# Keys' 32 rotary columns on the four quarters of the output, and the first loads in smaller pieces

## What is computed

```python
h = x @ w_in[l]                       # mla_cq 256, mla_ckv 128, mla_kr 32 columns among them
c = _rmsnorm(ckv, kv_norm)
k_rope = _rope(kr, cos, sin)          # t1*cos - t2*sin, t1*sin + t2*cos, shared by all heads
k = (mem @ w_k).reshape(B, M, MEM_HEADS, MEM_HDIM)
```

## Time and profile before

| what | value |
|---|---|
| runs shown | 1431.75, 1429.74, 1429.59 us; median 1429.74 |
| the profiled execution, its own time | 1432.5 us |
| its span, first to last instruction | 1430.7 us |
| mean granted PE clock | 0.964 |
| PE busy | 1283.5 us, 90% |
| DVE / ACT / POOL busy | 815.5 / 412.4 / 644.0 us |
| bytes moved | 407.8 MB, 268.5 of them by the gather |

### The profile page before, as it was taken

One profiled execution on the slowest core, in us unless ns is written; L12 is line 12 of the kernel. 1 busy time (PEld: TensorE's weight loads), 2 busy tenths in 40 slices (PEclk: granted clock), 3 DMA queues, 4 the chain that ended last, 5 costly groups with the idle time before them and its releaser, 6 DMA issues.

```text
span 1430.7 us, 17532 instructions
## 1 busy us (share of the span) xinstructions
PE 1283.5 (90%) x6312; PEld 790.5 (55%) x6312; DVE 815.5 (57%) x1681; ACT 412.4 (29%) x1032; POOL 644.0 (45%) x643
## 2 busy tenths in 40 slices
PE   9999999999999999999997899958977778787786
PEld 8877686548876686549556556523323333332332
DVE  0766377341566377351438756789797654544555
ACT  0532344111333333221322333322322231212123
POOL 0566667332537666433103344444644454444440
PEclk9999999999999999999999999978988989999999
DMA  9544334265453344365537999999999999999995
GB/s 379 192 163 178 118 141 184 110 262 198 152 184 155 118 177 175 134 229 196 203 151 270 413 419 412 420 420 420 420 419 420 420 421 419 421 420 419 421 420 209
DMA packets 53600, 407.82 MB, mean 285 GB/s; under 512 B 6133, under 2 KB 8586, under 8 KB 10890
## 3 DMA queue, kind: packets, MB, share of 16 engines
q0 software_dynamic: 36864, 268.45, 45.5%
q1 hardware_dynamic: 15562, 137.21, 24.9%
q10 hardware_dynamic: 1088, 1.05, 0.4%
HBM read 404.56 MB, written 1.07 MB: 284 GB/s over the span
## 4 chain that ended last, share of the span: by engine, by line
PE 39%; DMA 24%; DVE 7%; issue 3%; POOL 3%; ACT 3%; ACTq 0%; POOLq 0%; DVEq 0%
PE pj L675 13%; PE bank L1100 10%; DMA ring<-in_peer_uv,vM 9%; PE pj L711 5%; DMA yT<-in_peer_uv,vM 5%; DMA hv<-in_peer_uv,vM 3%; PE pj L690 3%; DMA more_rows<-in_peer_uv,vM 3%; DMA qM<-in_peer_uv,vM 3%; PE pj L970 2%; POOL more_rows L598 1%; DVE tri L1852 1%; PE bank L644 1%; POOL mod_part L599 1%; DMA qvE<-in_peer_uv,vM 1%
## 5 line engine op out<-in xcount | busy, mean ns | idle before, releaser
L675 PE MATMUL pj<-xT,ring 128*128 128x256 f32 (+2 forms) x1600 | 328.9, 366 | 0.9 <-ACT hv L1258 0.4
L675 PEld LDWEIGHTS pj<-xT,ring 128*128 128x128 f32 (+1 forms) x1600 | 282.2, 190 | 41.3 <-issue 3.6
L598 POOL TENSOR_SCALAR more_rows<-more_rows,lbt 128x256 f32<-128x256 f32 x168 | 174.9, 1041 | 16.4
L632 POOL DMA_INDIRECT ring<-in_peer_uv,vM x101 | 120.6, 1194 | 121.9 <-PE bank L1100 111.3
L596 POOL TENSOR_SCALAR mod_part<-more_rows,lbt 128x256 f32<-128x256 f32 x24 | 27.0, 1125 | 258.5 <-issue 112.2
L711 PE MATMUL pj<-ring,yT 128*128 128x512 f32 x320 | 141.3, 595 | 0.0
L599 POOL TENSOR_TENSOR mod_part<-mod_part,more_rows 128x256 f32<-128x256 f32 x168 | 128.6, 766 | 14.0
L1318 ACT ACTIVATE rope<-vM 128x4 f32<-128x4 f32 (+3 forms) x84 | 17.1, 204 | 406.3 <-DVE big L1852 323.5
L1100 PE MATMUL bank<-ring,causal 128*128 128x512 f32 x200 | 100.5, 642 | 19.4 <-ACT causal L1326 19.4
L1100 PE MATMUL bank<-ring,tri 128*128 128x512 f32 x204 | 97.6, 618 | 19.4 <-ACT tri L1326 19.4
L711 PEld LDWEIGHTS pj<-ring,yT 128*128 128x128 f32 x320 | 59.5, 190 | 69.4 <-issue 69.2
(11 more groups left out here) (368 smaller groups left out, 2106.1 us busy)
## 6 DMA issues: line engine op xcount, KB each, us to landing
ring<-in_units SPq DMA_DIRECT2D x44, 2048.0 KB, 9.5
more_rows<-in_w_ada SPq DMA_DIRECT2D x24, 1024.0 KB, 4.9
ring<-in_units SPq DMA_DIRECT2D x2, 1536.0 KB, 6.4
ring<-in_peer_uv,vM POOLq DMA_INDIRECT x101, 23.3
memT<-in_mem SPq DMA_DIRECT2D x1, 1024.0 KB, 5.0
ring<-in_units SPq DMA_DIRECT2D x2, 512.0 KB, 6.2
ring<-in_units SPq DMA_DIRECT2D x1, 1024.0 KB, 8.7
xT<-in_x_turned SPq DMA_DIRECT2D x1, 1024.0 KB, 10.5
```

The source lines that it names most:

```text
L598: do(g.tensor_scalar(mod_w[:, c, :], mod_w[:, c, :], silu_c[:, c:c + 1], None, ALU.mult))
L632: pool.indirect_dma_start(row_slot[k], None, d["peer_uv_2"], bass.IndirectOffsetOnAxis(ap=expert[:, t, j:j + 1], axis=0))\
L675: ins = nc.tensor.matmul(pj[s][0:n, 2 * m + first:2 * m + stop], ring[:, slot, at:at + n], act[:, c, first:stop], start=(c == 0), stop=(c ...
```

## The change

Memory is loaded in two halves of its chunks, and the first unit's first half in three pieces (256, 256 and 512 KB), in the order memory 0, first 0, memory 1, first 1, first 2. The first block's products wait for memory and weights twice, ahead of chunk 0 and ahead of chunk 4. WARM goes from 14 to 12, which is 24 records. In C (both layers) the product of chunk c for the 32 rotary columns writes output quarter c % 4, two chunks to a quarter; the four partial sums lie on partitions 0 to 127. ACT copies the whole tile at once. KR has two products with 128-row matrices: one swaps, signs and sums the quarters, one only sums them, and DVE reads both from the bank. `rot` has 65 columns for 33.

```diff
-WARM = 14
+WARM = 12
...
-    rot = np.zeros((P, 33), np.float32)
-    rot[:, 32] = np.where(i % 32 < 16, -1.0, 1.0)
+    rot = np.zeros((P, 65), np.float32)
+    rot[i, 32 + i % 32] = 1.0
+    rot[:, 64] = np.where(i % 32 < 16, -1.0, 1.0)
     for j in range(16):
-        for base in (0, 64):
+        for base in range(0, P, 32):
...
-            load(flat(memT), d["mem"], "mem_load")
+            MEM_HALF = DC // 2 * T
+
+            def mem(half):
+
+                c = slice(half * MEM_HALF, (half + 1) * MEM_HALF)
+                load(flat(memT)[:, c], d["mem"][:, c], f"mem_load{half}")
+
+            mem(0)
...
                 if n == 0:
                     first = width // 2
-                    for k in range(2):
-                        c = slice(k * width // 4, (k + 1) * width // 4)
-                        load(ring[:, slot, c], d["units"][n, :, c], f"first_load{k}")
+                    for k, (c0, c1) in enumerate(((0, width // 8), (width // 8, width // 4), (width // 4, width // 2))):
+                        load(ring[:, slot, c0:c1], d["units"][n, :, c0:c1], f"first_load{k}")
+                        if k == 0:
+                            mem(1)
...
                 for m in columns:
                     n = min(P, width - m)
-                    if UNIT[l, name] == 0 and part == "a":
-                        pe.wait_ge(sem(f"first_load{m // P}"), 16)
+                    if n == 32:
+                        for c in range(DC):
+                            k = 32 * (c % 4)
+                            ins = nc.tensor.matmul(pj[s][k:k + 32, 2 * m:2 * m + T], ring[:, slot, c * COLS + m:c * COLS + m + 32],
+                                                   act[:, c, :], start=(c < 4), stop=(c >= 4))
+                        continue
+                    if UNIT[l, name] == 0 and m == P:
+                        pe.wait_ge(sem("first_load2"), 16)
...
                     for c in chunks:
                         at = m * DC + c * P if UNIT[l, name] == 0 else c * COLS + m
+                        if UNIT[l, name] == 0 and m == 0 and c % (DC // 2) == 0:
+                            pe.wait_ge(sem(f"mem_load{2 * c // DC}"), 16)
+                            pe.wait_ge(sem(f"first_load{2 * c // DC}"), 16)
...
-                        last(nc.tensor.matmul(bank_of(key)[0:32, 0:T], rot[0:32, 0:32], cT[0:32, 3, :],
-                                              start=True, stop=True))
+                        for k in range(2):
+                            ins = nc.tensor.matmul(bank_of(key)[0:32, k * T:(k + 1) * T], rot[:, 32 * k:32 * k + 32],
+                                                   cT[:, 3, :], start=True, stop=True)
+                        last(ins)
...
-                        do(a.copy(cT[0:32, 3, :], pj[s][0:32, 3 * T:4 * T]))
-                        do(a.copy(cT[:, 0:3, :].rearrange("p a t -> p (a t)"), pj[s][:, 0:3 * T]), *freed(l, task))
+                        do(a.copy(flat(cT), pj[s][:, :]), *freed(l, task))
...
-                        do(v.tensor_tensor(tmp, bank_of(key)[0:32, 0:T], sin[0:32, :], ALU.mult), *bank_free(key))
-                        do(v.tensor_tensor(cT[0:32, 3, :], cT[0:32, 3, :], cos[0:32, :], ALU.mult))
+                        do(v.tensor_tensor(tmp, bank_of(key)[0:32, 0:T], sin[0:32, :], ALU.mult))
+                        do(v.tensor_tensor(cT[0:32, 3, :], bank_of(key)[0:32, T:2 * T], cos[0:32, :], ALU.mult),
+                           *bank_free(key))
```

More of the change, by code:

```diff
@@ L312, in build @@
         ones_mean = sb("ones_mean", [P, P])
-        rot = sb("rot", [P, 33])
+        rot = sb("rot", [P, 65])
         level_mask = sb("level_mask", [P, 7, P], u8)
@@ L872, in _ @@
                     elif name == "MK":
-                        pe.wait_ge(sem("mem_load"), 16)
                         channel_major(l, name, memT, COLS, part, (COLS - P,) if part == "c" else None)
@@ L1484, in _ @@
             cos, sin = rope[:, 0, :], rope[:, 1, :]
-            do(v.tensor_scalar(rope[96:P, 0, :], rope[96:P, 1, :], rot[96:P, 32:33], None, ALU.mult))
+            do(v.tensor_scalar(rope[96:P, 0, :], rope[96:P, 1, :], rot[96:P, 64:65], None, ALU.mult))
             def refine(y, mean, e, tmp, scale=1.0, free=None):
```

## The result

The changed kernel took 1421.41 us (median of 4 runs, 1420.36 to 1422.70) beside 1429.88 us for the kernel before on the same chip (4 runs): a ratio of 0.9937, 95% interval 0.9924 to 0.9950.

A forecast was written before the change was run, and what follows sets the result against it. TensorE (PE), busy 90% of the span, was taken to bound the kernel, with the expert-row gather behind it starting earlier by whatever PE gains. Terms -1.1 - 5.2 + 0.9 = -5.4 us gave 1424.3 us, range 1421.5 to 1428.0.

The forecast's parts named there:

- The quarters of C: C's 32 rotary columns in both layers: four quarters run at once, 3.65 us become 1.03 per layer, -5.2 us.
- Rival A: C's 32 columns: only two quarters run at once, 1.1 us more per layer, 1426.5 us in all; 12%.
- KR: KR's one product becomes two, one behind the other: 0.44 us more per layer, +0.9 us.
- ACT's copy: Two copies (0.36 + 0.80 us) become one of 0.80 to 1.16 us, for which no one waits: term 0.
- DVE's cosine product: Behind KR, it reads PSUM in place of SBUF, 0.41 us for one and 0.51 for the other: 0.
- The start: Smaller first pieces and 24 warming records: first product at about 6.0 us in place of 7.12, -1.1 us.
- 768 KB are there at 5.0 us: At the start: the first memory and weight pieces land by then, so warming and not data sets the first product.
- Rival C: At the start: pieces land late, PE idles 1 us and its clock falls, 1439.4 us; 5% with all other slower ways.
- The constants: Loading at the start: rotation constants grow by 16 KB, which was taken to cost nothing.
- The clock: Behind PE's 2.00 us wait the clock halves, costing 1.7 us; a shift may make a drop come or go.
- Rival B: No change: quarters don't overlap for long streams, or the gain is swallowed downstream, as in the gather; 1429.5 us, 17%.

The follow-up runs named there:

- e1_start: Kernel before with only the start of the change (memory in halves, first weights in three pieces, WARM 12): 1429.87 us, ratio 0.9998.
- f1_before_fill: Kernel before with nine idle products ahead of P0 in both layers, where PE waits 2.0 us: 1427.97 us, ratio 0.9986.
- f2: Changed kernel with nine idle products ahead of P0 in both layers: 1421.48 us, ratio 0.9939 to the kernel before.
- h4_fill_rot105: Changed kernel with nine idle products ahead of P0 and a 105-column rot tile (65 loaded): 1413.15 us, ratio 0.9880 to the kernel before.
- i3_all_slots_0: h4_fill_rot105 with spacer tiles that move more_rows to a multiple of 256 bytes as well: 1411.67 us, ratio 0.9876 to the kernel before.

## Why the prediction was off

- **The quarters of C, -5.2 forecast.** Right: 3.65 us became 1.07 in each layer, -2.56 in the table and the same 1.07 in every profile with the edit, where 0.9 + 0.13 = 1.03 was forecast; four quarters run at once. Rival A, two at a time, gave 1.98 + 0.13 for that stretch, and is refuted by the 1.07.
- **KR, +0.9 forecast.** Right: the group went from 1.2 to 2.1 us, and the path lost 0.34 us in layer 0 between C and the scores. ACT's copy (1.01 us) and DVE's cosine product (0.41 for 0.51) cost nothing, as forecast.
- **The start, -1.1 forecast.** Right at the first product (-1.06) and too large where it counts: 0.9, 0.7, 0.4 and 0.2 us at C in four profiles. The step that failed in it is "768 KB are there at 5.0 us": the small pieces came as late as 6.1, and the second pair at 8.5 in place of 7.1. Why they come late is not shown. Rival C did not come: the short waits for weights, 0.32 and 0.38 us in e1_start, have no fall of the clock behind them, since the 56 records from 8.47 take 12.32 us, 0.220 each. Even the full 1 us of idling that it needs has none behind it, in f1_before_fill, where warming ended early:

```profile
1.30 4.87 PE L698 MATMUL pj<-ones_mean 128*128 128x128 f32 x28 [1.30 <-DVE ones_mean L1446]
7.18 14.05 PE L675 MATMUL pj<-memT,ring 128*128 128x256 f32 x64 [1.01 <-DMA ring<-in_units]
```

- **The constants, 0 forecast.** This is the step that put the forecast off: "Rotation constants grow by 16 KB: nothing." It priced the transfer and not the shift of every tile behind the constants. Measured alone it is -1.9 us. With it the terms are, at the start measured, -0.2 to -0.9 - 5.1 + 0.9 - 1.9 = -6.3 to -7.0, beside 6.9 between f1 and f2.
- **The clock, 1.7 on both sides.** The size was right (1.68), and it was seen as something that a shift makes come or go. It comes and goes without any shift too, by the counts above about as often after as before, so that one drop fewer in the profiled pair needs no other cause than chance. With the two absent waits (0.90; that stretch of the table takes 160.7 to 161.6 us in the profiles with C as before, and in those with C on quarters too, so it varies by itself) it makes up most of what the spans' 9.8 us have over the runs' 7.5.

Rival B (no change) is refuted too: what was gained ahead of the gather arrived at it in full, -7.64 at modulation's last stretch and -7.65 at the first gather.

The best version was not the changed kernel but h4_fill_rot105, 1413.15 us, and i3_all_slots_0 at 1411.67: the change, nine idle products in PE's one long wait, and the tiles behind `rot` on multiples of 256 bytes.

## What to carry to other kernels

Small products that fill a fraction of the output's partitions belong round its quarters: here 16 records that cost 3.5 us cost 1.1, for one more product that sums the parts. When a constant tile changes its width, look where everything behind it starts: a gather that keeps the DMA engines full gained 1.7% when the tiles behind started on multiples of 256 bytes, more than the edit under study. And when an effect is a few us, compare the start of one and the same instruction in several profiles of each kernel before giving a difference a cause, since a clock drop of 1.7 us may stand in one execution and not in the next.

## What the runs showed of the hardware that was not expected

- The gather's rate by the place of the tiles behind `rot` within 256 bytes: 420 GB/s at 32 and 224, 422 at 96 and 128, 427 at 0, with the DMA engines full in all. A packet of 8 KB takes 314.8, 313.9 and 309.3 ns at 224, 96 and 0. One destination of fifteen that stood at 96 while the others stood at 0 cost nothing.
- The granted clock after one and the same 2.0 us wait: mean 0.67 over the next 5 us in one execution, 1.00 in another. It fell behind 19 of 26 such waits. With idle products in the wait it fell behind none of eight.
- The warming products' pace rises at a different moment in different executions: 28 records in 4.87 to 6.32 us.
